# S5 recurrence of layer 0: two tokens per step, with half the phase table and a direct term

## The chip, the cores and the metric

The kernel runs on one core of one Trainium2 chip. The metric is the device time of one execution in microseconds (us). Before the change it is 1573.44 us, the median of three runs (1571.39, 1573.44, 1573.77).

## The reference, cut to what matters

Two layers of a decoder trunk on 256 tokens of width 1024, all in float32. The change touches one part of layer 0, the S5 mixer: 32 groups of 16 channels, each with 64 complex states.

```
dt = exp(log_dt); mag = exp(a_re * dt); abar = mag * (cos(a_im*dt) + i sin(a_im*dt))   # per group and state
bbar = ((abar - 1) / a) * b                                                            # 64 states x 16 channels
x[s] = abar * x[s-1] + bbar @ u[s]                                                     # s = 0..255, complex
y[s] = Re(c @ x[s]) + d_skip * u[s]
y    = gelu(y);  out = y * sigmoid(y @ w_glu + b_glu)
```

`u` is the last quarter of one combined input projection; its other three quarters are q, k and v of eight attention heads. The outputs of attention and S5 are concatenated and go into one output projection; a dense SwiGLU follows, then layer 1 (sparse attention and a mixture of eight experts).

## The kernel before, in words

Every engine has a queue of its own, written out by hand in program order, with semaphores between the queues. The 32 x 64 states lie as 16 channel tiles (`NCH`) of 128 partitions: two groups of 64 states each. PE is TensorE, DVE VectorE, ACT ScalarE, POOL GpSimd.

**Phase table.** The rotation of the state is taken out of the recurrence. `phase` holds cos and sin of s times the angle for each tile and token, 16 x 256 each. DVE builds it in eight doublings, `level(0)` to `level(7)` (L2185 to L2194, six operations each); a doubling needs the next power of the rotation, which POOL squares in `power(n)`. In the middle of the last doubling DVE computes the modulation (`columns`) and half of the first normalised input `uT` (`norm_first_out`); ACT does the other half.

**Weights.** POOL forms `b_bar`, ACT spreads it and c block-diagonally into `b_pad` and `c_pad`, PE transposes these (`s5_transposes`, 16 transposes of 128 x 128, before the projection), and ACT copies the results to `s5_bT` and `s5_cT` (`s5_weights`).

**The stage of the recurrence.** PE's order: `s_proj(0..3)` projects the S5 inputs (16 channels x 8 groups = 128 rows each, 256 tokens); then eight blocks, each with six matmuls of the q, k, v projection (`qkv`, 128x512), `drive` of two tiles, and `read_out` of the two tiles before. For each tile j:

- `drive(j)` on PE: 2 matmuls (real and imaginary) of a 32-row slice of the input, 256 tokens, to one PSUM bank (three banks in turn);
- `turn(j)` on DVE: two multiplies of 128x512 by the phase, an add and a subtract (the rotation back), and two scans over 256 tokens with factor `mag`;
- on POOL: two multiplies of 128x512 by the phase (L818), the rotation forward;
- `read_out(j)` on PE: 4 matmuls of 128 rows to 32 output rows, 256 tokens; those of two tiles alternate and lie in different column strips of the array.

`y_before_gelu(t)` on DVE adds `d_skip * u` for four tiles at once. DVE also does the rotary part of q and k (`rope0`) between turns. After the last block PE transposes q and k (`qk_transposes`), computes the first scores (L958), then `read_out(14)`, more scores, and `glu()` (L1127), which waits for the gelu of all four y tiles on ACT.

In the profile each float32 matmul of this stage stands as two records; a transpose stands as one. x8 at the drive is thus four matmuls.

## Time and profile before

| | |
|---|---|
| median of three runs | 1573.44 us |
| span of the profiled execution | 1566.3 us |
| what lies around the span, against that median | 7.1 us |
| PE busy in the span | 1489.2 us (95%) |
| DVE busy | 1288.4 us (82%) |
| ACT busy | 1027.9 us (66%) |
| POOL busy | 113.8 us (7%) |
| mean granted clock of PE | 0.986 of full |

The span is the time from the first to the last instruction that the hardware profiler recorded; the shares are of it. The table says nothing of single stages. The stage that the change touches runs from about 43 us to 137 us of the span.

### The profile page before, as it was taken

Reading aid. Unit: us, or ns where it says so; the run is one execution under the profiler, and the core shown is the slowest. Engines: PE = TensorE matmul, PEld = TensorE weight load, DVE = VectorE, ACT = ScalarE, POOL = GpSimd, SP = SyncE. Lnnn points to the kernel's source line nnn. Section 1 sums busy time; section 2 is a strip of 40 time slices with the busy share of each in tenths; the row PEclk is TensorE's granted clock in tenths of the full one; section 3 lists DMA queues with packets and bytes.
Section 4 is the critical chain, followed back from the end, with each engine's and each line's share of the span. In section 5 each row is a group of like instructions: output and inputs, shape, how many; then the busy total and the mean of one; then the engine's idle time right before and its main releaser. Section 6 shows DMA issues by size and latency. Waiting matters only on the chain.

```text
span 1566.3 us, 21687 instructions
## 1 busy us (share of the span) xinstructions
PE 1489.2 (95%) x7201; PEld 1160.6 (74%) x7202; DVE 1288.4 (82%) x1776; ACT 1027.9 (66%) x1325; POOL 113.8 (7%) x112
## 2 busy tenths in 40 slices
PE   3999999999899899999999999999999999999987
PEld 1645468888795478878888888888888888888865
DVE  6896458785586369899999999989989989989987
ACT  3104444443456457887787788787888888888765
POOL 5251000000000000000001001001001001001030
PEclk9899999999899999999999999999999999999998
DMA  9733968874564289999999999999999999999960
GB/s 309 274 108 138 386 253 294 310 257 161 190 215 164 106 315 392 389 339 386 386 348 384 390 346 379 389 356 373 384 358 373 385 365 368 387 365 367 383 232 28
DMA packets 209930, 482.81 MB, mean 308 GB/s; under 512 B 8084, under 2 KB 14534, under 8 KB 209750
## 3 DMA queue, kind: packets, MB, share of 16 engines
q1 hardware_dynamic: 205872, 468.91, 81.3%
q0 software_dynamic: 3360, 12.10, 2.1%
q10 hardware_dynamic: 646, 1.16, 0.3%
q8 instruction: 27, 0.44, 0.1%
q14 instruction: 25, 0.20, 0.0%
HBM read 474.27 MB, written 7.86 MB: 308 GB/s over the span
## 4 chain that ended last, share of the span: by engine, by line
PE 80%; DVE 5%; ACT 4%; issue 2%; DVEq 0%; ACTq 0%
PE ps L864 23%; PE ps L866 23%; PE ps L865 23%; PE ps L870 3%; DVE w_lo L2056 3%; PE ps L1399 2%; PE ps L1156 2%; ACT work L1947 1%; PE ps L889 1%; ACT w_hi L1686 1%; PE ps L1127 0%; PE ps L958 0%; PE ps L1345 0%; ACT uT L1699 0%; PE ps L984 0%
## 5 line engine op out<-in xcount | busy, mean ns | idle before, releaser
L2056 DVE TENSOR_TENSOR w_lo<-ring,w_hi 128x1024 fp32r<-128x1024 f32 (+2 forms) x572 | 676.5, 1214 | 80.6 <-ACT w_hi L1686 61.7
L1686 ACT ACTIVATE w_hi<-ring 128x1024 fp32r<-128x1024 f32 (+2 forms) x572 | 596.0, 1052 | 222.6 <-PE ps L866 220.6
L864 PE MATMUL ps<-w_hi,e_hi 128*128 128x512 f32 x896 | 356.2, 398 | 5.5 <-DVE w_lo L2056 5.5
L866 PE MATMUL ps<-w_hi,e_lo 128*128 128x512 f32 x896 | 349.5, 390 | 0.0
L865 PE MATMUL ps<-w_lo,e_hi 128*128 128x512 f32 x896 | 348.8, 389 | 0.0
L2056 DVE TENSOR_TENSOR w_lo<-ring_more,w_hi 128x1024 fp32r<-128x1024 f32 x192 | 232.1, 1223 | 16.0 <-ACT w_hi L1686 7.0
L1686 ACT ACTIVATE w_hi<-ring_more 128x1024 fp32r<-128x1024 f32 x192 | 202.7, 1060 | 47.6 <-PE ps L866 47.6
L864 PEld LDWEIGHTS ps<-w_hi,e_hi 128*128 128x128 f32 x896 | 168.3, 188 | 42.1 <-DVE w_lo L2056 9.6
L866 PEld LDWEIGHTS ps<-w_hi,e_lo 128*128 128x128 f32 x896 | 168.1, 188 | 36.1
L865 PEld LDWEIGHTS ps<-w_lo,e_hi 128*128 128x128 f32 x896 | 168.5, 188 | 32.7
L864 PE MATMUL ps<-w_hi,eT_hi 128*128 128x512 f32 x448 | 176.7, 395 | 12.6 <-DVE w_lo L2056 12.6
L866 PE MATMUL ps<-w_hi,eT_lo 128*128 128x512 f32 x448 | 174.6, 390 | 0.0
L865 PE MATMUL ps<-w_lo,eT_hi 128*128 128x512 f32 x448 | 174.5, 390 | 0.0
L864 PEld LDWEIGHTS ps<-w_hi,eT_hi 128*128 128x128 f32 x448 | 84.0, 188 | 35.5 <-DVE w_lo L2056 18.7
L864 PE MATMUL ps<-w_hi,x_hi 128*128 128x512 f32 (+4 forms) x272 | 99.9, 367 | 4.6 <-DVE x_lo L2091 4.6
L866 PE MATMUL ps<-w_hi,x_lo 128*128 128x512 f32 (+4 forms) x272 | 98.7, 363 | 0.0
L865 PE MATMUL ps<-w_lo,x_hi 128*128 128x512 f32 (+4 forms) x272 | 98.5, 362 | 0.0
L866 PEld LDWEIGHTS ps<-w_hi,eT_lo 128*128 128x128 f32 x448 | 84.1, 188 | 17.9
L865 PEld LDWEIGHTS ps<-w_lo,eT_hi 128*128 128x128 f32 x448 | 84.2, 188 | 16.7
L864 PEld LDWEIGHTS ps<-w_hi,x_hi 128*128 128x128 f32 x272 | 51.6, 190 | 13.6 <-issue 6.7
L834 POOL DMA_INDIRECT y_rows<-work,y_index x7 | 27.9, 3988 | 430.7 <-DVE work L2634 430.7
L865 PEld LDWEIGHTS ps<-w_lo,x_hi 128*128 128x128 f32 x272 | 51.7, 190 | 7.0
(308 smaller groups left out, 1579.8 us busy)
## 6 DMA issues: line engine op xcount, KB each, us to landing
ring<-in_moe_w_gate SPq DMA_DIRECT2D x96, 1024.0 KB, 7.2
ring<-in_moe_w_up SPq DMA_DIRECT2D x80, 1024.0 KB, 7.2
ring<-in_moe_w_down SPq DMA_DIRECT2D x64, 1024.0 KB, 7.2
ring<-in_w_ada SPq DMA_DIRECT2D x24, 2048.0 KB, 12.6
ring_more<-in_moe_w_down SPq DMA_DIRECT2D x48, 1024.0 KB, 7.5
ring_more<-in_moe_w_up SPq DMA_DIRECT2D x32, 1024.0 KB, 7.6
ring_more<-in_moe_w_gate SPq DMA_DIRECT2D x16, 1024.0 KB, 7.6
ring<-in_ff_w_gate SPq DMA_DIRECT2D x5, 2048.0 KB, 8.2
```

The lines of the kernel that those rows point to most:

```text
L834: pool.indirect_dma_start(y_rows[:, :], bass.IndirectOffsetOnAxis(ap=y_index[:, 0:1], axis=0), y_sb, None).then_inc(y_stored, 16)
L864: mm(o, xh, wh, start=start, stop=False)
L865: mm(o, xh, wl, start=False, stop=False)
L866: return mm(o, xl, wh, start=False, stop=stop)
L870: return nc.tensor.transpose(o, i, ident[0:n, 0:n])
L889: w = mm(ps[bank][j:j + 32, :], c_col[:, k:k + 1].broadcast_to([P, 32]), ap[:, k, :], start=k < 4, stop=False, tile_position=(0, j))
L1156: w = mm(ps[2 * n + t][:, :], catT[:, k, t * P:(t + 1) * P], ap[:, k, :], start=k == 4, stop=k == 3)
L1399: w = mm(ps[4 + 2 * n + t][:, :], ctxT[:, k, t * P:(t + 1) * P], ap[:, k, :], start=k == 0, stop=k == KD - 1)
L1686: fn(w, src, ACT.Copy).then_inc(hi_ready, 1)
L1947: w = fn(x_e[:, k, :], ps[6 + i][:, (k % 4) * P:(k % 4 + 1) * P], ACT.Identity, scale=mod_a[:, 1, k:k + 1], bias=mod_b[:, 1, k:k + 1])
L2056: V.tensor_tensor(w_lo[0:n, c, 0:f], src, w_hi[0:n, c, 0:f].bitcast(F32), ALU.subtract).then_inc(lo_ready, 1)
```

## The change

The recurrence is written for two tokens at a time: x[2k+1] = A^2 x[2k-1] + (A B) u[2k] + B u[2k+1]. Only odd states are kept. Odd outputs are C x[2k+1] as before; even outputs are y[2k] = (C A) x[2k-1] + (C B) u[2k], whose second part is the "direct term".

- The phase table has 128 steps instead of 256, so seven doublings; `level(n)` takes the next power, `n + 1`. The modulation and `norm_first_out` stand behind the last doubling.
- Two channel tiles (j and j+4) go together: eight turns `jp` instead of 16. A turn on DVE has the same four operations of 128x512 elements in all, and four scans of 128 steps instead of two of 256. POOL's two multiplies per turn keep their size, and there are eight pairs instead of 16.
- `drive(jp)`: eight matmuls of 128 tokens, all in the same 32-row strip of the array (`s5_abT` on even inputs, `s5_bT` on odd ones). Blocks 0 to 5 issue one each.
- `read_out(jp0)` serves four channel tiles: 36 matmuls of 127 or 128 tokens, two column strips in turn. It is issued four times instead of eight.
- New: `s5_direct` on PE (eight matmuls of 128x128), copied out by four small operations of ACT; `ab_bar` on POOL and its copy `ab_pads` on ACT; eight more transposes; three C A weight tiles made on POOL (seven operations of 128x512).
- `s5_transposes` moves from ahead of `s_proj(0)` to behind `s_proj(1)`, with 24 transposes.

```diff
-        phase = phase_buf[:, :, :].rearrange("p a (b c) -> p a b c", b=NCH)
+        phase = phase_buf[:, 0, :].rearrange("p (a b c) -> p a b c", a=2, b=NCH)
...
             for n in range(5, NLEV - 1):
                 power(n)
...
+            for i, (x, y, op) in enumerate(((0, 1, ALU.subtract), (1, 0, ALU.add))):
+                mul(s5_t, f(AI), b_bar[:, y, :, :])
+                mul(ab_bar[:, i, :, :], f(AR), b_bar[:, x, :, :])
...
+            pool.wait_ge(s5_wT_ready, 5)
...
+            mul(ca_t, fw(AI), mci)
+            mul(ca[0], fw(AR), cr)
+            add(ca[0], ca[0], ca_t)
+            affine(ca[1], ca[0], -1.0, 0.0)
+            mul(ca_t, fw(AI), cr)
+            mul(ca[2], fw(AR), mci)
...
-                for i, bank in enumerate((5, 6, 7, 4)):
+                for i, bank in enumerate((5, 6, 7, 4, 5, 6)):
                     if i == 3:
                         pe.wait_ge(mod_ready, 1)
+                    if i == 4:
+                        pe.wait_ge(s5_pads, 12)
+                        pe.wait_ge(s5_wT_ready, 2)
...
             pe.wait_ge(part_ready, 4)
-            s5_transposes()
             pe.wait_ge(uT_ready, 8)
...
+            def s5_direct():
+
+                pe.wait_ge(s5_wT_ready, 5)
+                for t in range(4):
+                    o = ps[7][:, t * P:(t + 1) * P]
+                    mm(o, b_pad[:, 0, t, :], s5_cT[:, 0, t, :], start=True, stop=False)
+                    w = mm(o, b_pad[:, 1, t, :], s5_cT[:, 2, t, :], start=False, stop=True)
+                w.then_inc(k_done, 1)
...
+            def drive(jp):
...
+                for n, j in enumerate(j_pair(jp)):
+                    t, r = j // 4, slice(32 * (j % 4), 32 * (j % 4) + 32)
+                    u = halves_of(t, r)
+                    for i in range(2):
+                        o = bank[:, (2 * n + i) * HS:(2 * n + i + 1) * HS]
+                        mm(o, s5_abT[r, i, t, :], u[:, 0, :], start=True, stop=False, tile_position=(r.start, 0))
+                        w = mm(o, s5_bT[r, i, t, :], u[:, 1, :], start=False, stop=True, tile_position=(r.start, 0))
                 w.then_inc(bu_done, 1)
...
+            def read_out(jp0):
...
+                for n in range(2):
...
+                    for jp in pairs:
+                        r, o = at_(jp, 0)
+                        mm(o, s5_kT[:, t, r], halves_of(t, slice(0, P))[:, 0, :], start=True, stop=False, tile_position=(0, r.start))
+                    for i, (c, a, b) in enumerate(((0, 0, 0), (1, 1, 1), (2, 1, 0), (2, 0, 1))):
+                        for jp in pairs:
...
+                            mm(o, s5_caT[:, c, t, r], x[:, 0:HS - 1], start=False, stop=i == 3, tile_position=(0, r.start))
+                    for i, (c, a, b) in enumerate(((0, 0, 0), (1, 1, 1), (2, 1, 0), (2, 0, 1))):
+                        for jp in pairs:
...
+                            w = mm(o, s5_cT[:, c, t, r], x, start=i == 0, stop=i == 3, tile_position=(0, r.start))
...
             s_proj(0)
             s_proj(1)
+            s5_transposes()
             s_proj(2)
+            s5_direct()
             drive(0)
-            drive(1)
             s_proj(3)
             pending[0] = True
-            drive(2)
-            for jp in range(8):
-                for s in range(6 * jp, 6 * jp + 6):
+            drive(1)
+            for i in range(8):
+                for s in range(6 * i, 6 * i + 6):
                     qkv(s)
-                for j in (2 * jp + 3, 2 * jp + 4):
-                    if j < NCH:
-                        drive(j)
-                if jp:
-                    read_out(2 * jp - 2)
+                if i + 2 < NJP:
+                    drive(i + 2)
+                if i in (2, 4, 6):
+                    read_out(i - 2)
...
             scores_pair(0, qT, kT, 0, True)
-            read_out(NCH - 2)
+            read_out(NJP - 2)
...
-            for n in range(5, NLEV):
+            for n in range(5, NLEV - 1):
                 level(n)
+            columns(0, 0, 1, 4)
+            dve.wait_ge(mod_ready, 1)
+            norm_first_out()
...
+                for n, j in enumerate(j_pair(jp)):
+                    for i in range(2):
+                        w = V.tensor_tensor_scan(z[:, n, i, :], s5_p[:, MAG2, j:j + 1].broadcast_to([P, HS]), s5_v2[:, n, i, :],
+                                                 0.0, ALU.mult, ALU.add)
...
-            for j in range(NCH):
-                turn(j)
-                if j % 4 == 2 and j >= 6:
-                    y_before_gelu(j // 4 - 1)
-                if j in (7, 8, 12, 13):
-                    rope0({7: 0, 8: 1, 12: 2, 13: 3}[j])
+            for jp in range(NJP):
+                turn(jp)
+                if jp in (3, 4):
+                    rope0(jp - 3)
+                if jp == 6:
+                    y_before_gelu(0)
+                    y_before_gelu(1)
+                if jp in (6, 7):
+                    rope0(jp - 4)
             dve.wait_ge(tables_in, 16)
             mask_max(0, neg0)
             mask_max(1, neg0)
+            y_before_gelu(2)
             y_before_gelu(3)
```

PE's order at the start of the stage, before. The rows are the last modulation columns (x1), the transposes of the S5 weights, the S5 projection (`uT,ring`, 256 tokens), the drives (`ada,work`) and the first six `qkv` matmuls (`ring,uT`); here x4 counts matmuls.

```order
L903 MATMUL ps<-cst,ada 128x1 x8
L870 MATMUL ps<-cst,work 128x128 x16
L1018 MATMUL ps<-uT,ring 128x256 x24
L1054 MATMUL ps<-ada,work 128x256 x4
L1018 MATMUL ps<-uT,ring 128x256 x8
L1054 MATMUL ps<-ada,work 128x256 x2
L1036 MATMUL ps<-ring,uT 128x512 x6
```

The same place after the change; L1092 and L1093 are the first of the four pairs of `s5_direct`, and the last two rows the first of the four pairs of `drive(0)`.

```order
L948 MATMUL ps<-cst,ada 128x1 x8
L1062 MATMUL ps<-uT,ring 128x256 x16
L912 MATMUL ps<-cst,work 128x128 x16
L912 MATMUL ps<-cst,phase_buf 128x128 x8
L1062 MATMUL ps<-uT,ring 128x256 x8
L1092 MATMUL ps<-work 128x128
L1093 MATMUL ps<-work 128x128
...
L1115 MATMUL ps<-ada,phase_buf 128x128
L1116 MATMUL ps<-ada,work 128x128
```

The 16 transposes moved behind two thirds of the first projection, eight more and `s5_direct` came in, and only one drive stands ahead of the last projection.

PE's order in two consecutive blocks of the middle, before (L1067 is the read-out, to 32 rows).

```order
L1036 MATMUL ps<-ring,uT 128x512 x6
L1054 MATMUL ps<-ada,work 128x256 x4
L1067 MATMUL ps<-gate_row,work 32x256 x8
L1036 MATMUL ps<-ring,uT 128x512 x6
L1054 MATMUL ps<-ada,work 128x256 x4
L1067 MATMUL ps<-ada,work 32x256 x8
```

After, the block with the first read-out, from the last pair of its drive to the next block.

```order
L1115 MATMUL ps<-ada,phase_buf 128x128
L1116 MATMUL ps<-ada,work 128x128
L1137 MATMUL ps<-ada,work 32x128 x2
L1142 MATMUL ps<-ada,phase_buf 32x127 x8
L1147 MATMUL ps<-ada,work 32x128 x8
L1137 MATMUL ps<-ada,work 32x128 x2
L1142 MATMUL ps<-ada,phase_buf 32x127 x8
L1147 MATMUL ps<-ada,work 32x128 x8
L1080 MATMUL ps<-ring,uT 128x512 x6
```

The read-out of eight matmuls in every block became one of 36, half as long each, in every second block.

## Rows read from the trace of the kernel before

**Rows 1.** Windows of the span: busy time by engine, PE's granted clock, DMA.

```profile
64.00:128.00 64.00, 62.53 (x245) 28.13 (x244) 59.78 (x110) 3.15 (x6) 34.37 (x29) 1.00 0.29 99
```

**Rows 2.** PE's timeline: start, duration, line, operation, count, idle before and releaser.

```profile
62.93 1.12 PE L1054 MATMUL ps<-ada,work 32*128 32x256 f32 x4
63.99 5.42 PE L1036 MATMUL ps<-ring,uT 128*128 128x512 f32 x12
...
75.75 1.14 PE L1054 MATMUL ps<-ada,work 32*128 32x256 f32 x8
76.82 1.92 PE L1067 MATMUL ps<-ada,work 128*32 128x256 f32 x16
78.67 5.42 PE L1036 MATMUL ps<-ring,uT 128*128 128x512 f32 x12
84.02 1.14 PE L1054 MATMUL ps<-ada,work 32*128 32x256 f32 x8
...
102.35 1.12 PE L1054 MATMUL ps<-ada,work 32*128 32x256 f32 x4 [0.67 <-DVE work L2242]
...
128.28 1.92 PE L1067 MATMUL ps<-ada,work 128*32 128x256 f32 x16 [1.08 <-DVE work L2258]
```

**Rows 3.** PE's timeline ahead of the S5 projection.

```profile
39.95 3.58 PE L903 MATMUL ps<-cst,ada 128*128 128x1 f32 x16
43.39 3.65 PE L870 MATMUL ps<-cst,work 128*128 128x128 f32 x16
47.31 10.97 PE L1018 MATMUL ps<-uT,ring 128*128 128x256 f32 x48 [0.27 <-ACT uT L1661]
```

**Rows 4.** DVE's timeline: last doubling's second operation, and its half of uT.

```profile
42.73 2.28 DVE L2186 TENSOR_TENSOR phase_buf<-phase_buf,work 128x2048 f32<-128x2048 f32 x1
...
45.32 1.90 DVE L2075 TENSOR_SCALAR uT<-ps,mod_a,mod_b 128x256 f32<-128x256 f32 x4
```

**Rows 5.** Windows at the start of the stage, for PE's granted clock (third number from the end).

```profile
46.00:48.00 2.00, 1.73 (x7) 1.24 (x7) 2.00 (x4) 2.00 (x5) 0.00 (x0) 0.50 1.05 387
48.00:50.00 2.00, 2.00 (x11) 1.77 (x10) 1.97 (x2) 1.69 (x4) 0.00 (x0) 0.99 1.05 389
```

**Rows 6.** A later return to the full clock: PE's timeline row and a window.

```profile
564.41 0.60 PE L1434 MATMUL ps<-bias_rows,cst 128*128 128x8 f32 x2 [1.09 <-DVE bias_rows L2489]
```

```profile
570.00:571.00 1.00, 1.00 (x10) 1.00 (x10) 1.00 (x1) 0.38 (x2) 0.00 (x0) 0.86 1.05 399
```

**Rows 7.** PE's short matmuls elsewhere; the last row gives duration ns as min/median/max.

```profile
130.13 1.09 PE L870 MATMUL ps<-cst,work 128*128 128x128 f32 x8
...
151.19 0.88 PE L984 MATMUL ps<-uT,ada 128*64 128x128 f32 x12
152.00 1.05 PE L903 MATMUL ps<-cst,work 128*128 128x1 f32 x8
...
555.75 2.25 PE L1404 MATMUL ps<-cst 128*128 128x128 f32 x18
```

```profile
L1404 PE MATMUL ps<-cst x50: 275/275/561, 555.7 to 574.3; 128*128 128x128 f32 x50
```

**Rows 8.** Timelines of DVE (first turn) and POOL (one tile).

```profile
59.38 0.69 DVE L2239 TENSOR_TENSOR work<-ps,phase_buf 128x512 f32<-128x512 f32 x1 [3.10 <-PE ps L1054]
...
61.70 1.27 DVE L2249 TENSOR_TENSOR_SCAN work<-work 128x256 f32<-128x256 f32 x2
```

```profile
66.81 2.50 POOL L818 TENSOR_TENSOR ada<-work,phase_buf 128x512 f32<-128x512 f32 x2 [1.21 <-DVE work L2249]
```

**Rows 9.** Timelines of PE and DVE from the last read-out to the GLU.

```profile
134.32 1.92 PE L1067 MATMUL ps<-gate_row,work 128*32 128x256 f32 x16
136.19 0.93 PE L958 MATMUL ps<-ada 64*128 64x128 f32 x8
137.30 7.17 PE L1127 MATMUL ps<-work,ring 128*128 128x256 f32 x32 [0.18 <-ACT work L1749]
```

```profile
136.31 0.48 DVE L2258 SCALAR_TENSOR_TENSOR work<-ada,s_d,ps 128x256 f32<-128x256 f32 x1 [0.18 <-PE ps L1067]
```

More of the change, by code:

```diff
@@ L239, in trunk @@
         s5_v = W0.take(2, S)
-        s5_small = W0.take(10)
         powers = W0.take(NLEV, 2, NCH)
+        s5_kT = W0.take(4, P)
         WA = Region(ada, 6 * D)
@@ L257, in trunk @@
         pT = WU.take(2, KW)
-        phase = phase_buf[:, :, :].rearrange("p a (b c) -> p a b c", b=NCH)
+        phase = phase_buf[:, 0, :].rearrange("p (a b c) -> p a b c", a=2, b=NCH)
+        WS = Region(phase_buf[:, 1, :], SLOT)
+        s5_abT = WS.take(2, 4, P)
+        s5_caT = WS.take(3, 4, P)
+        ab_pad = WS.take(2, 4, P)
+        ab_bar = WS.take(2, NCH, C_S5)
         WI = Region(ada[:, 2 * 4 * S:2 * 4 * S + 2048], 2048)
@@ L296, in trunk @@
         late_in = sem("late_in")
-        fill = [sem(f"slot{i}_filled") for i in range(NS1)]
+        fill = [sem(f"slot{i}_filled") for i in range(NS0)]
         half_fill = [[sem(f"slot{i}_half{j}_filled") for j in range(2)] for i in range(NS1)]
@@ L775, in _ @@
             step(pool.memset(b_pad, 0.0))
+            step(pool.memset(ab_pad, 0.0))
+            step(pool.memset(s5_kT, 0.0))
             step(pool.memset(phase[:, 0, :, 0:1], 1.0))
@@ L1047, in drive, with halves_of @@
+            def halves_of(t, r):
+                return s_inT[r, t, :].rearrange("p (k l) -> p l k", l=2)
+            def drive(jp):
+                if jp == 0:
+                    pe.wait_ge(s5_wT_ready, 7)
                     pe.wait_ge(vs_ready, 1)
-                if j == 8:
+                if jp == 4:
                     pe.wait_ge(vs_ready, 2)
-                if j >= 3:
-                    pe.wait_ge(bu_used, j - 2)
-                r = slice(32 * (j % 4), 32 * (j % 4) + 32)
-                for i in range(2):
-                    w = mm(ps[(6, 4, 5)[j % 3]][:, i * S:(i + 1) * S], s5_bT[r, i, j // 4, :], s_inT[r, j // 4, :], start=True,
-                           stop=True, tile_position=(32 * (j % 4), 0))
@@ L1056, in drive @@
[L1056 to L1070 removed]
+                if jp >= 3:
+                    pe.wait_ge(bu_used, jp - 2)
@@ L1729, in _, with s_in_out @@
             norm_first_out()
-            s5_weights()
-            act.wait_ge(s5_pads, 8)
-            for i in range(2):
+            ab_pads()
+            act.wait_ge(s5_pads, 12)
+            def s_in_out(i):
                 act.wait_ge(proj_done, 1 + i)
                 fn(s_inT[:, 2 * i:2 * i + 2, :], ps[2 + i][:, :].rearrange("p (c s) -> p c s", c=2), ACT.Copy).then_inc(vs_ready, 1)
+            s_in_out(0)
+            s5_weights(range(7))
+            s5_direct_out()
+            s_in_out(1)
             for i in range(4):
@@ L2238, in turn @@
                 step.wait()
[L2239 to L2242 removed]
+                chained(V.tensor_tensor(rotB, bu, phase_of(1, jp), ALU.mult))
+                chained(V.tensor_tensor(bu, bu, phase_of(0, jp), ALU.mult))
@@ L2243, in turn @@
+                step(V.tensor_tensor(s5_v2[:, :, 0, :], bu[:, :, 0, :], rotB[:, :, 1, :], ALU.add))
+                V.tensor_tensor(s5_v2[:, :, 1, :], bu[:, :, 1, :], rotB[:, :, 0, :], ALU.subtract).then_inc(bu_used, 1)
                 step.wait()
-                dve.wait_ge(bu_used, j + 1)
-                if j >= 2:
-                    dve.wait_ge(post_ready, j - 1)
-                z = zbuf[:, j % 2]
-                for i in range(2):
-                    w = V.tensor_tensor_scan(z[:, i, :], s5_p[:, MAG, j:j + 1].broadcast_to([P, S]), s5_v[:, i, :],
-                                             0.0, ALU.mult, ALU.add)
-                    if i == 0:
-                        step(w)
+                dve.wait_ge(bu_used, jp + 1)
@@ L2253, in turn @@
+                if jp >= 2:
+                    dve.wait_ge(post_ready, jp - 1)
+                z = zbuf[:, jp % 2]
+                for n, j in enumerate(j_pair(jp)):
+                    for i in range(2):
+                        w = V.tensor_tensor_scan(z[:, n, i, :], s5_p[:, MAG2, j:j + 1].broadcast_to([P, HS]), s5_v2[:, n, i, :],
+                                                 0.0, ALU.mult, ALU.add)
+                        if (n, i) != (1, 1):
+                            step(w)
                 w.then_inc(z_ready, 1)
-                dve.wait_ge(z_ready, j + 1)
+                dve.wait_ge(z_ready, jp + 1)
```

145 lines of the change are left out of this document (86 added, 59 removed).

## The prediction

> **What bounds the kernel now.** I read the windows by stage first, then PE's timeline in the stage of the recurrence, then DVE's and ACT's beside it. In the 64 us of [rows 1] PE is busy 62.53 us and DVE 59.78 us. Both look full, and the page alone would let one believe that DVE's scans set the pace. PE's timeline decides it: each group of six `qkv` matmuls is followed at once by a drive, that by a read-out, that by the next six [rows 2]. From 63.99 us, where the blocks begin, to 130.13 us [rows 7], where the q transposes follow the last read-out of the blocks, PE waited twice: 0.67 us for a PSUM bank and 1.08 us for y [rows 2]. That is all that DVE costs there: 1.75 us. So PE's own work is the bound, and DVE is a little less than full beside it. What the change takes from DVE gives at most those 1.75 us; what it adds to PE counts in full.
>
> Ahead of the stage, the projection starts at 47.31 us and waits for `uT` [rows 3]. DVE's half of `uT` runs from 45.32 us, after an operation of the last doubling that ends at 42.73 + 2.28 = 45.01 us [rows 4]; but the modulation columns were summed at 39.95 + 3.58 = 43.53 us [rows 3]. So the last doubling holds the path for about 1.5 us. Its other operations lie behind `uT` and beside PE's projection.
>
> **Prices.** A drive of two tiles costs PE 76.82 - 75.75 = 1.07 us, that of a single tile 63.99 - 62.93 = 1.06 us [rows 2]. Two tiles cost no more than one: they lie in different 32-row strips and run side by side. A read-out costs 78.67 - 76.82 = 1.85 us for 16 records in two column strips, that is eight steps of 0.23 us [rows 2]. So four records of a single drive stream for 0.92 us, and about 0.14 us goes to the change of shape.
>
> No row shows a 128-token float32 matmul in a 32-row or 32-column strip. The nearest is the full-array one: 18 records in 2.25 us, the last of which alone lasts 0.275 us, so (2.25 - 0.275) / 17 = 0.116 us each [rows 7]. That is half of 0.23, so the weight load still hides at 128 tokens. In column strips of 64 the step is (152.00 - 151.19) / 6 = 0.135 us, change of shape included [rows 7]. The lower bound is half of 0.23 less its fixed part, about 0.107; the upper bound inside this mechanism is 0.135. I take 0.116. A transpose costs (1.09 - 0.27) / 7 = 0.117 us [rows 7].
>
> **The change on PE, term by term.**
>
> - Transposes. The 16 old ones ran from 43.39 to 47.04 us, while PE would have waited for `uT` anyway: they cost nothing there. Behind `s_proj(1)` they are on the path: 16 x 0.117 = +1.9 us. The eight new ones: +0.9 us. They need two weight copies of ACT first; these take about as long as the first 16, so I add no wait.
> - `s5_direct`: eight matmuls, 16 records x 0.116 = +1.9 us.
> - Drives. Before: six pairs at 1.07 and four single ones at 1.06, together 10.7 us without the wait. After: each of the eight has 16 records in one row strip, so nothing runs side by side: 16 x 0.116 + 0.14 = 2.0 us, together 16.0. Difference +5.3 us. Tokens streamed are the same; the strips that ran together are lost.
> - Read-outs. Before 8 x 1.85 = 14.8 us. After 36 matmuls in two column strips make 18 steps of two records: 36 x 0.116 + 0.1 = 4.3 us, four times 17.2. Difference +2.4 us; the direct term is what is added.
> - The two waits for DVE: -1.75 us. DVE then has eight turns of some 3.6 us (61.70 + 1.27 - 59.38, [rows 8]; four scans of 128 for two of 256, which even at twice the price of a step leave a turn under 5 us), against a block of PE of 7 to 12 us. Banks come free long before the drive that reuses them.
> - Start of the projection: -1.45 us, from 47.31 to about 45.9 us, as the modulation starts at 43.6 instead of 45.05.
> - Clock. PE's granted clock is 0.50, the 1.2 GHz level, when the projection starts, and back at the full level at 48.0 us [rows 5]: the 0.7 us at half cost 0.35. Before, PE had worked without a gap from about 40 us to then. Now it stands idle from 43.5 to 45.9 us. After such a gap at the half level it worked from 564.41 us to about 570.3 us until the clock came back, 5.9 us [rows 6]. I take 4.7 us, between 0.7 and 5.9 but nearer to the row with a gap: 2.35 us lost instead of 0.35, +2.0 us. With the earlier start together: +0.55 us (from -1.4 to +1.2).
> - End. Only the last read-out now completes y(2) and y(3), so two additions and two gelus stand behind it instead of one; the chain from its end at 136.19 to the GLU at 137.30 [rows 9] grows by one addition less its overlap, +0.4 us.
>
> Off the path: POOL's C A tiles are seven operations at 2.50 / 2 = 1.25 us [rows 8], about 9 us, ready long before the first read-out, some 36 us behind `s_proj(1)`. POOL's `ab_bar` and ACT's copies end before the projections do. DVE's first doublings start about 1 us later, as they need the next power; the slack behind the shorter table takes it. The two DMA queues carry nothing new, and PE waits for no load in the stage. If POOL's C A were not covered, the first read-out would stall PE by what is missing, up to 9 us.
>
> Sum: 1.9 + 0.9 + 1.9 + 5.3 + 2.4 - 1.75 + 0.55 + 0.4 = +11.6 us. Everything behind the GLU is shifted by that and not changed; PE is as full there. The profiled span of 1566.3 us becomes 1577.9, and with the 7.1 us that the median of the runs has over that span, **1585.0 us**, 0.7% slower.
>
> **A rule against the row.** The single drive speaks for hidden loads: four records with 128-column weights in one row strip in 1.06 us [rows 2], while 128-column loads with next to no stream are spaced up to 1.05 / 8 = 0.13 us [rows 7]; were load and stream in series, the four would take 4 x (0.12 + 0.23) = 1.4 us. The Trainium skill, "TensorE: Matmul & The Clock Gate", Part 3, says that a weight load overlaps matmuls in flight only when its row group differs, while its Part 2 also allows the background weight buffer. By Part 3 the new drives, all in one row group, would pay every load; that is the first rival.
>
> **Rivals.**
>
> 1. *Loads in series in one row strip.* With half the stream per load there is less to hide it behind. Each record of a drive then costs 0.116 + 0.12 = 0.24 us, a drive 3.9 us, eight of them 15 us more: about 1600 us. Against it: the 1.06 us row and the 0.116 us row. Chance 0.08.
> 2. *Faster: the small tiles run beside the `qkv` matmuls.* The drives and read-outs take a quarter of the array. If PE's queue overlapped them with the full-array matmuls, their columns would cost little and DVE's 59.78 busy us in [rows 1] would have been the pace; halving its turns would let the blocks close up to their `qkv` part, by up to 15 us, about 1560 us. It decides from the point where more than 12 us of the 33 us of drives and read-outs is hidden. Against it: each drive and read-out pushes the next `qkv` group by its full length [rows 2]. Chance 0.04.
> 3. *No change.* Part of the same overlap, or 7 us and more of added work in PE's idle moments around the start. PE has only some 2 us idle there. Chance 0.04.
> 4. *Clock at half through all the transposes.* If it came back only behind them, the projections and the 24 transposes would lose about 3 us more than I took: 1588 us. Inside the range.
>
> **How the numbers follow.** The forecast has a chance of 0.84, including the fourth rival. Its own range: with 0.107 us a record 2 us less, with 0.135 us 5 us more, the start from -2 to +3 us, and 1 us for the median of a few runs: 1580 to 1592. I put the range at 1579 to 1593. A measurement of this kernel can tell about 0.2%, 3 us. Faster: 0.04 and a remainder, 0.05. Same: 0.04. Slower: 0.91.
>
> **What the profile of the changed kernel would show.** Each drive 2.0 us from its start to the next group (3.9 if the first rival holds); each read-out 4.3 us; the `qkv` groups still 5.35 us; PE without waits between the blocks, while DVE waits for PE before most turns; the projection starting at about 45.9 us with the clock at 0.50 for some us; the GLU starting near 149 us instead of 137.30. The prediction is wrong if `qkv` groups start before the drive ahead of them has had its time, if a drive costs near 1.1 us, or if DVE's turns still stand ahead of waiting PE work.

## The result and the profile after

The changed kernel took 1582.17 us (median of five runs, 1576.90 to 1585.69), the kernel before 1573.44 us (1571.39 to 1573.77). The ratio is 1.0056, with a 95% interval of 1.0038 to 1.0074: slower by 0.6%. The forecast was 1585.0 us with a range of 1579 to 1593.

| | before | after |
|---|---|---|
| median | 1573.44 us | 1582.17 us |
| profiled execution: time / span | not listed / 1566.3 us | 1584.64 / 1582.8 us |
| PE busy | 1489.2 us | 1505.6 us |
| DVE busy | 1288.4 us | 1247.0 us |
| mean granted clock of PE | 0.986 | 0.980 |
| start of the GLU of layer 0 | 137.30 us [rows 9] | 147.79 us |

DVE lost 41 us of work in the whole span and the kernel became slower. The windows of the changed kernel say why at once; the columns are those of [rows 1]:

```profile
46.00:48.00 2.00, 2.00 (x5) 1.64 (x6) 0.00 (x0) 1.37 (x4) 0.00 (x0) 0.50 1.04 385
48.00:50.00 2.00, 2.00 (x6) 1.55 (x6) 0.00 (x0) 0.00 (x0) 0.00 (x0) 0.50 1.05 389
50.00:52.00 2.00, 2.00 (x9) 1.73 (x8) 0.00 (x0) 0.00 (x0) 0.00 (x0) 0.84 1.04 385
...
64.00:128.00 64.00, 64.00 (x369) 40.57 (x368) 35.54 (x87) 3.83 (x9) 20.64 (x18) 1.00 0.29 99
```

In the last row DVE's work fell from 59.78 to 35.54 us, and PE went from 62.53 us to all of the 64. The first three answer to [rows 5]: the clock is at 0.50, the 1.2 GHz level, from the start of the projection until 50 + 2 x (1 - 0.84) / 0.5 = 50.64 us.

PE's timeline of the changed kernel, from the modulation columns to the GLU (L948 columns, L912 transposes, L1062 projection, L1092 and L1093 direct term, L1115 and L1116 drive, L1080 `qkv`, L1137 to L1147 read-out, L1206 GLU):

```profile
39.76 2.25 PE L948 MATMUL ps<-cst,ada 128*128 128x1 f32 x16
45.94 9.47 PE L1062 MATMUL ps<-uT,ring 128*128 128x256 f32 x32 [3.94 <-issue]
55.24 1.91 PE L912 MATMUL ps<-cst,work 128*128 128x128 f32 x16
57.23 1.07 PE L912 MATMUL ps<-cst,phase_buf 128*128 128x128 f32 x8
58.13 3.62 PE L1062 MATMUL ps<-uT,ring 128*128 128x256 f32 x16
61.59 0.38 PE L1092 MATMUL ps<-work 128*128 128x128 f32 x2
...
63.46 0.49 PE L1115 MATMUL ps<-ada,phase_buf 32*128 32x128 f32 x2
...
65.47 3.72 PE L1062 MATMUL ps<-uT,ring 128*128 128x256 f32 x16
...
71.13 5.42 PE L1080 MATMUL ps<-ring,uT 128*128 128x512 f32 x12
76.48 0.49 PE L1115 MATMUL ps<-ada,phase_buf 32*128 32x128 f32 x2
...
78.48 5.42 PE L1080 MATMUL ps<-ring,uT 128*128 128x512 f32 x12
...
93.19 0.42 PE L1137 MATMUL ps<-ada,work 128*32 128x128 f32 x4
93.45 1.03 PE L1142 MATMUL ps<-ada,phase_buf 128*32 128x127 f32 x16
94.31 1.04 PE L1147 MATMUL ps<-ada,work 128*32 128x128 f32 x16
...
97.25 1.12 PE L1080 MATMUL ps<-ring,uT 128*128 128x512 f32 x2
...
146.28 0.93 PE L1003 MATMUL ps<-ada 64*128 64x128 f32 x8
147.79 2.42 PE L1206 MATMUL ps<-work,ring 128*128 128x256 f32 x10 [0.59 <-ACT work L1852]
```

A piece of work costs the time from its start to the start of the next piece. A drive is 65.47 - 63.46 = 2.01 us, and again 78.48 - 76.48 = 2.00; the `qkv` group is still 76.48 - 71.13 = 5.35 us; a read-out is 97.25 - 93.19 = 4.06 us for twice 4 + 16 + 16 = 72 records. No piece of the blocks has a wait ahead of it. It is DVE that waits now. The list of DVE's waits has this for the first operation of its turn (us in total, times, longest; the longest is the first, ahead of the blocks):

```profile
DVE work L2339 <- PE ps L1116: 44.5, 8, 19.8
```

Ahead of the projection, DVE's timeline of the changed kernel:

```profile
38.44 1.63 DVE L2289 TENSOR_TENSOR phase_buf<-phase_buf,ada 128x1024 f32<-128x1024 f32 x1
40.10 1.23 DVE L2290 TENSOR_TENSOR ada<-phase_buf,work 128x1024 f32<-128x1024 f32 x1
...
42.50 1.23 DVE L2292 TENSOR_TENSOR phase_buf<-phase_buf,ada 128x1024 f32<-128x1024 f32 x1
43.64 0.15 DVE L2149 COPY mod_b<-ps 128x8 f32<-128x8 f32 x1
...
43.91 1.90 DVE L2178 TENSOR_SCALAR uT<-ps,mod_a,mod_b 128x256 f32<-128x256 f32 x4
```

The columns were summed on PE at 39.76 + 2.25 = 42.01 us, but DVE came to them only at 43.64, when its last doubling was done. So DVE, not the columns, still held the path. Beside its doublings POOL did the new work for `ab_bar` (L769, L833), which lasted until 37.40 + 1.58 = 38.98 us:

```profile
35.84 1.49 POOL L769 TENSOR_TENSOR phase_buf<-work,ada 128x256 f32<-128x256 f32 x1
37.40 1.58 POOL L833 TENSOR_TENSOR phase_buf<-phase_buf,ada 128x256 f32<-128x256 f32 x1
```

DVE's operations of 128x1024 beside these took 1.53, 1.64 and 1.63 us, the two behind them 1.23 and 1.22. The kernel before has no such work on POOL, and 1.22 us for this size.

**The numbers behind the GLU.** The GLU starts 10.49 us later. The profiled span is 16.5 us longer and the medians differ by 8.7 us. What lies behind the GLU took 1566.3 - 137.30 = 1429.0 us before and 1582.8 - 147.79 = 1435.0 after, at a lower mean clock. The same kernel repeats that spread: the five runs of the changed kernel have spans of 1575.1 to 1583.9 us at clocks of 0.988 to 0.980. The start of the GLU is the sharper measure of each edit, and each experiment gives both.

It has a spread of its own, for it is read from one execution of each kernel. The changed kernel and three of its edited versions below (drives by twos, read-out of four strips, DVE padded) have the same code up to the end of the first 32 projection records; that end comes at 55.24, 55.64, 54.72 and 55.31 us, as the clock comes back sooner or later. Three traces (the kernel before and its two edited versions) have the same code up to the first block. In them the 48 projection records start within 0.05 us of each other and take 10.97, 12.24 and 13.20 us, and the first block starts at 63.99 us (the trace of [rows 2]), 65.20 and 66.19 us. So the GLU of the changed kernel is known to about 1 us and that of the kernel before to about 2, and the trace of the kernel before that was read for the prediction was the luckiest of the three. That fits a median that moved by 8.7 us where the GLU moved by 10.49.

### The profile page after: what moved, and what is told of

Read it like the earlier page. It is cut to its first block, busy times and chain, and to the rows that moved or that the text cites. A ratio compares the mean times of both kernels' runs of the same rounds, so it can differ in the third digit from the quotient of the medians.

```text
span 1582.8 us, 22130 instructions
## 1 busy us (share of the span) xinstructions
PE 1505.6 (95%) x7449; PEld 1183.5 (75%) x7450; DVE 1247.0 (79%) x1738; ACT 1031.8 (65%) x1335; POOL 108.7 (7%) x112
## 4 chain that ended last, share of the span: by engine, by line
PE 86%; DVE 5%; ACT 4%; issue 2%; DMA 1%; SPq 1%; DVEq 0%; ACTq 0%
PE ps L906 23%; PE ps L908 22%; PE ps L907 22%; PE ps L912 3%; PE ps L1080 3%; DVE w_lo L2159 3%; PE ps L1478 2%; PE ps L1235 2%; PE ps L934 1%; ACT work L2050 1%; DMA ring<-in_w_ada 1%; PE ps L1062 1%; SPq L658 1%; ACT w_hi L1782 1%; PE ps L1115 1%
## 5 line engine op out<-in xcount | busy, mean ns | idle before, releaser
L906 PE MATMUL ps<-w_hi,eT_hi 128*128 128x512 f32 x448 | 177.7, 397 | 10.8 <-DVE w_lo L2159 10.8
L908 PEld LDWEIGHTS ps<-w_hi,x_lo 128*128 128x128 f32 x272 | 52.3, 192 | 7.3
```

Source lines behind the costliest of these rows:

```text
L906: mm(o, xh, wh, start=start, stop=False)
L908: return mm(o, xl, wh, start=False, stop=stop)
```

## The experiments

My theory: PE's own work sets the pace of the stage, DVE has slack after the change, and the time lost lies in small matmuls that use one row strip (drives) or two column strips (read-outs) where more could run side by side. The rivals: DVE's turns, or a wait hidden in PE's row, set the pace; and, for the start of the stage, that the clock after PE's gap, not DVE's doublings, is what costs.

All but two experiments (the kernel before with DVE padded, and with a read-out of four strips) edit the changed kernel. Each stands beside fresh runs of the kernel before, whose medians were 1573.04, 1572.85 and 1574.09 us in the three sets.

| | median | ratio to before, 95% | GLU starts |
|---|---|---|---|
| drives by twos | 1570.70 us | 0.9998, 0.9979 to 1.0016 | 139.39 us |
| transposes ahead | 1579.38 us | 1.0042, 1.0022 to 1.0062 | 145.25 us |
| read-out of four strips | 1572.88 us | 1.0004, 0.9986 to 1.0022 | 139.06 us |
| all three | 1558.83 us | 0.9922, 0.9898 to 0.9947 | 128.23 us |
| changed kernel, DVE padded | 1581.25 us | 1.0050, 1.0031 to 1.0069 | 147.85 us |
| before, DVE padded | 1581.06 us | 1.0051, 1.0029 to 1.0072 | 147.44 us |
| fill in the gap | 1580.89 us | 1.0051, 1.0033 to 1.0070 | 147.69 us |
| all three, `uT` first | 1556.38 us | 0.9884, 0.9864 to 0.9905 | 124.95 us |
| before, read-out of four strips | 1579.96 us | 1.0047, 1.0030 to 1.0065 | 148.42 us |

### Drives by twos

Two turns' drives are issued together, their matmuls in turn, so that neighbours lie in different row strips and different banks.

```diff
-            def drive(jp):
+            def drive(*jps):
...
-                for n, j in enumerate(j_pair(jp)):
...
-                        mm(o, s5_abT[r, i, t, :], u[:, 0, :], start=True, stop=False, tile_position=(r.start, 0))
-                        w = mm(o, s5_bT[r, i, t, :], u[:, 1, :], start=False, stop=True, tile_position=(r.start, 0))
+                for n in range(2):
+                    for i in range(2):
+                        for k, (wT, first) in enumerate(((s5_abT, True), (s5_bT, False))):
+                            for jp in jps:
+                                j = j_pair(jp)[n]
...
+                                w = mm(o, wT[r, i, t, :], halves_of(t, r)[:, k, :], start=first, stop=not first,
+                                       tile_position=(r.start, 0))
...
-            drive(0)
+            drive(0, 1)
             s_proj(3)
-            drive(1)
...
-                if i + 2 < NJP:
-                    drive(i + 2)
+                if i in (0, 2, 4):
+                    drive(i + 2, i + 3)
```

> The changed kernel with its drives issued in twos, the matmuls of two turns in different 32-row strips alternating, nothing else. My theory (PE's own work is the bound, and the drives lost their side-by-side strips): two drives take the 2.0 us of one, so 8 us leave the stage; the GLU starts at about 139.8 us of the span instead of 147.79, and the time falls from 1582 to about 1574. Rival (weights or the order of the queue set the price, not the strips): two drives take 4 us and nothing changes. Rival (DVE paces the stage): nothing changes.

PE's timeline of this kernel, with the columns and the projection first, and four records in a row of the drives where the changed kernel has two:

```profile
38.36 1.95 PE L948 MATMUL ps<-cst,ada 128*128 128x1 f32 x16
...
46.05 9.75 PE L1062 MATMUL ps<-uT,ring 128*128 128x256 f32 x32 [5.74 <-ACT uT L1758]
...
63.85 0.50 PE L1116 MATMUL ps<-ada,phase_buf 32*128 32x128 f32 x4
...
65.86 3.72 PE L1062 MATMUL ps<-uT,ring 128*128 128x256 f32 x16
```

Two drives take 65.86 - 63.85 = 2.01 us, exactly what one took. Four calls instead of eight save 8.0 us; the GLU comes 147.79 - 139.39 = 8.40 us earlier, although the first 32 projection records had ended 0.4 us later than in the changed kernel. So the drives' excess was the lost side-by-side work, as the prediction had it. The Trainium skill, "TensorE: Matmul & The Clock Gate", Part 3, also has it that tiles in different strips run at once, and this run agrees with that.

The first two rows bear on the start of the stage: here the columns were summed at 40.31 us, 1.7 us earlier than in the changed kernel, and the projection started at 46.05 all the same. The columns are not what it waits for.

### Transposes ahead

```diff
+            s5_transposes(range(4))
             pe.wait_ge(uT_ready, 8)
...
             s_proj(1)
-            s5_transposes()
+            s5_transposes((4, 5))
```

ACT's first five weight copies move ahead of its pads with them.

> The changed kernel with the 16 old transposes back ahead of the wait for uT. My theory: 1.9 us leave the path, and as PE works on through the gap, its clock comes back earlier than at 50.6 us, worth up to 2 us more: the GLU at 144 to 146 us. If the gap does not matter for the clock, only the 1.9 us: 145.9 us. Rival (the transposes were hidden where they are now): GLU stays at 147.8.

The projection now runs from 46.01 to 54.70 us and the eight remaining transposes follow; the GLU comes 2.54 us earlier than in the changed kernel. The 16 moved transposes had cost 1.99 us in the timeline above (57.23 - 55.24), the rest is the clock: the windows from 46, 48 and 50 us read 0.63, 0.52 and 1.00 where the changed kernel has 0.50, 0.50 and 0.84, which is 2 x (0.13 + 0.02 + 0.16) = 0.6 us. That those 0.6 us are the work of the edit is not shown: the next kernel has nothing changed ahead of the projection, and its first 32 records take 54.72 - 46.07 = 8.65 us, against 8.69 here and 9.30 in the changed kernel.

### Read-out of four strips

```diff
-                pairs = (jp0, jp0 + 1)
+                pairs = range(jp0, jp0 + 4)
...
-                if i in (2, 4, 6):
-                    read_out(i - 2)
+                if i == 2:
+                    read_out(0)
...
-            read_out(NJP - 2)
+            read_out(NJP - 4)
```

The wait for `post` grows from `jp0 + 2` to `jp0 + 4` turns. One call now covers four channel tiles, in all four column strips.

> The changed kernel with its four read-outs of two column strips made two read-outs of all four strips, same matmuls. My theory: a read-out's 18 steps take as long with four tiles as with two, 4.1 us, so two read-outs less, 8.1 us: GLU at about 139.7 us and about 1574 us. If the issue of 288 instructions is slower than the steps, a read-out takes up to 6 us and the gain is 4 us. Rival (PE waits for four turns of DVE and POOL before the read-out): a wait of several us ahead of the read-outs, and no gain.

The GLU comes 8.73 us earlier. Two calls of 4.06 us are 8.1 of them; 0.52 us stood already at the end of the first 32 projection records, ahead of anything edited. A row that shows such a read-out stands with the next experiment.

### All three

The three edits above together.

> The changed kernel with drives in twos, read-outs of four strips and the 16 transposes ahead of the wait for uT. If the terms add as PE's own work: 8 + 8.1 + 1.9 and up to 2 us less than the changed kernel, the GLU at 128 to 130 us of the span against 137.3 in the kernel before, and a time of 1564 to 1566 us, 0.5% under the kernel before. If DVE, POOL or the issue of PE become the bound once PE's work shrinks, the stage stops near the kernel before, GLU at 134 us or later.

PE's timeline of this kernel, the first row of a read-out of four strips and the `qkv` behind it; then its window for the stage:

```profile
86.25 0.43 PE L1141 MATMUL ps<-ada,work 128*32 128x128 f32 x8
...
90.31 1.99 PE L1082 MATMUL ps<-ring,uT 128*128 128x512 f32 x4
```

```profile
64.00:128.00 64.00, 62.34 (x525) 36.27 (x523) 39.05 (x101) 8.45 (x16) 20.03 (x16) 1.00 0.36 125
```

The read-out of twice the matmuls takes 90.31 - 86.25 = 4.06 us, the same as that of two strips. The three edits alone moved the GLU by 8.40 + 2.54 + 8.73 = 19.67 us, together by 147.79 - 128.23 = 19.56: they add up, as parts of a queue do when it alone is the bound. (To 0.1 us is luck, at a spread of about 1 us.) With them the halved recurrence is 0.8% faster than the kernel before. The time came out lower than expected: the median is 14.2 us under that of the kernel before, while the GLU starts only 137.30 - 128.23 = 9.07 us earlier. Where the other 5 us lie is open. PE executes exactly the same matmuls as in the changed kernel; only their order and neighbours differ.

### The changed kernel, DVE padded

The first multiplication of each turn is done three times: 8 x 2 more operations of 0.72 us, 11.5 us in all.

```diff
+                chained(V.tensor_tensor(rotB, bu, phase_of(1, jp), ALU.mult))
+                chained(V.tensor_tensor(rotB, bu, phase_of(1, jp), ALU.mult))
                 chained(V.tensor_tensor(rotB, bu, phase_of(1, jp), ALU.mult))
```

> The changed kernel with the first multiply of each turn on DVE issued three times instead of once: 16 more operations of 0.7 us, 11.6 us more on DVE in the stage, same results. My theory (PE is the bound and what DVE saves is slack): the GLU stays at 147.8 us and the time at 1582, within noise. Rival (DVE's turns pace the stage): 11 us later, 1593 us.

Its window for the stage:

```profile
64.00:128.00 64.00, 64.00 (x370) 40.60 (x369) 46.04 (x98) 3.89 (x9) 19.98 (x17) 1.00 0.28 99
```

DVE works 46.04 us instead of 35.54 in this window, and the GLU moves by 0.06 us. DVE does not bound the changed kernel; it has at least these 11.5 us of slack.

### The kernel before, DVE padded

The same 11.5 us (16 turns, one more operation each) in the kernel before.

```diff
+                chained(V.tensor_tensor(rotB, bu, c(1), ALU.mult))
                 chained(V.tensor_tensor(rotB, bu, c(1), ALU.mult))
```

> The kernel before with the first multiply of each of its 16 turns issued twice: 11.5 us more on DVE. This prices the slack that DVE had before. DVE was busy 59.8 of 64 us and PE waited 1.75 us for it in the stage, so I expect DVE to become the bound here: 6 to 9 us more, about 1580 us. If DVE had been the pace already, 11.5 us more, 1585 us; if its slack was larger than I read it, no change.

Two rows of PE's timeline and the window of the stage:

```profile
47.26 12.24 PE L1018 MATMUL ps<-uT,ring 128*128 128x256 f32 x48 [1.31 <-ACT uT L1661]
...
108.33 2.07 PE L1054 MATMUL ps<-ada,work 32*128 32x256 f32 x4 [4.59 <-DVE work L2243]
```

```profile
64.00:128.00 64.00, 59.41 (x218) 27.16 (x216) 60.63 (x109) 3.16 (x6) 32.50 (x26) 0.92 0.29 99
```

The GLU moves by 147.44 - 137.30 = 10.14 us. Of these, 65.20 - 63.99 = 1.21 us stood already at the first block, ahead of anything edited: the 48 projection records took 12.24 us instead of 10.97 [rows 3], as the clock came back later. The 11.5 us of work thus cost about 8.9 us, and the median moved by 8.2, at the upper end of what was expected. PE waits, and its clock falls: the drive behind the 4.59 us wait takes 2.07 us instead of 1.1. So before the change DVE had some 2.6 us of slack behind PE, known to about 2 us. The two directions are not alike: 11.5 us more on DVE cost about 9 us, and 24 us less gave back only the 1.75 us for which PE had waited [rows 2] and 1.06 us more, as the account of the prediction shows.

### Fill in the gap

Five dummy matmuls between the columns and the wait for `uT`, to hold the clock.

```diff
+            for _ in range(5):
+                mm(ps[5][:, 0:P], ident, ident, start=True, stop=True)
             pe.wait_ge(uT_ready, 8)
```

> The changed kernel with five dummy matmuls of 128x128 on PE between the modulation columns and the wait for uT, to an unused bank; they fill some 2 us of the gap. It asks what the gap alone costs through the clock. My theory: the granted clock is back to full earlier than at 50.6 us, and the first projection (45.94 to 55.24 us) ends up to 1.5 us earlier. Rival (the gap does not matter, or the dummies run past uT): no change or up to 0.5 us later.

PE's timeline and a window of this kernel:

```profile
40.03 1.36 PE L1055 MATMUL ps<-cst 128*128 128x128 f32 x10
46.61 8.70 PE L1064 MATMUL ps<-uT,ring 128*128 128x256 f32 x32 [5.22 <-ACT uT L1759]
```

```profile
46.00:48.00 2.00, 1.39 (x3) 1.17 (x4) 0.52 (x2) 1.93 (x6) 0.00 (x0) 0.50 1.03 383
```

The dummies end at 41.4 us, 5.22 us ahead of the projection, and the clock is at half all the same when it starts. The GLU moves by 0.10 us. DVE's doublings ran about 0.7 us later in this execution, already before the dummies, so that the projection started at 46.61 us instead of 45.94; in return the clock was back 3.25 us after that start, where it took 4.7 us in the changed kernel. Without dummies it took from 3.4 us (read-out of four strips) to 5.3 us (drives by twos). So no gain of the burst is shown, and one of under about 1 us is not ruled out. The gain of up to 1.5 us at the projection's end that was expected did not come: it ended at 55.14 us instead of 55.24.

### All three, uT first

The kernel with all three edits, and DVE's last doubling placed behind the columns and the first norm's output.

```diff
-            for n in range(5, NLEV - 1):
-                level(n)
+            level(5)
             columns(0, 0, 1, 4)
             dve.wait_ge(mod_ready, 1)
             norm_first_out()
+            level(6)
```

> The version with drives in twos, read-outs of four strips and the transposes ahead of uT, and in addition the modulation columns and uT ahead of the last doubling of the table instead of behind it. My theory: in the changed kernel it was DVE's doublings (up to 43.6 us) and no longer PE's columns (done near 40.2 us when the clock is full) that held uT; moved, the projection starts at 42.5 to 43 us instead of 46.1, or when its weights land, and the GLU at about 125 us instead of 128.23; time 1555 to 1556 us. Rival (the weights of the projection land only near 46 us): no gain. Rival (the last doubling, now later, delays the first turn): a wait of DVE's table ahead of the first turn.

PE's timeline of this kernel, then DVE's, then POOL's (L769 and L833 of 128x256 are the last of `ab_bar`):

```profile
41.91 1.95 PE L912 MATMUL ps<-cst,work 128*128 128x128 f32 x16
44.41 7.17 PE L1064 MATMUL ps<-uT,ring 128*128 128x256 f32 x32 [0.56 <-ACT uT L1760]
51.42 1.04 PE L912 MATMUL ps<-cst,phase_buf 128*128 128x128 f32 x8
```

```profile
42.15 0.17 DVE L2153 COPY mod_b<-ps 128x8 f32<-128x8 f32 x1 [6.64 <-PE ps L949]
...
46.63 1.23 DVE L2293 TENSOR_TENSOR phase_buf<-phase_buf,ada 128x1024 f32<-128x1024 f32 x1
47.89 1.95 DVE L2294 TENSOR_TENSOR ada<-phase_buf,work 128x1024 f32<-128x1024 f32 x1
49.77 2.06 DVE L2295 TENSOR_TENSOR phase_buf<-phase_buf,work 128x1024 f32<-128x1024 f32 x1
```

```profile
36.07 0.62 POOL L769 TENSOR_TENSOR phase_buf<-work,ada 128x256 f32<-128x256 f32 x1
36.77 0.72 POOL L833 TENSOR_TENSOR phase_buf<-phase_buf,ada 128x256 f32<-128x256 f32 x1
46.92 1.84 POOL L769 TENSOR_TENSOR work<-work 128x512 f32<-128x512 f32 x1 [9.43 <-issue]
48.84 1.91 POOL L769 TENSOR_TENSOR phase_buf<-work 128x512 f32<-128x512 f32 x1
...
54.60 1.05 POOL L769 TENSOR_TENSOR work<-work 128x512 f32<-128x512 f32 x1
```

The projection starts 1.5 us earlier than in the changed kernel, and takes 51.42 - 44.41 = 7.01 us where that took 55.24 - 45.94 = 9.30, at the full clock from its first matmul: PE's gap had shrunk to 0.56 us. The GLU comes 3.28 us before that of the kernel with three edits: 1.70 us by the start of the projection and 1.58 by its clock. This is the best version: 1556.38 us, 1.2% faster than before. DVE's doublings had thus held the projection in the changed kernel, and the clock behind the gap came with them. The start was expected at 42.5 to 43 us and came at 44.41: now the columns hold it, and DVE waited 6.64 us for them.

The rows of POOL show what had made the doublings slow. With DVE idle, the last two operations of `ab_bar` take 0.62 and 0.72 us; in the changed kernel, beside the doublings, they take 1.49 and 1.58. DVE's 128x1024 takes 1.22 us where POOL is idle and up to 1.64 beside them.

### The kernel before, read-out of four strips

Is it the four strips alone that gain, without the halved recurrence?

```diff
-                pe.wait_ge(post_ready, j0 + 2)
+                pe.wait_ge(post_ready, j0 + 4)
...
-                    for j in (j0, j0 + 1):
+                    for j in range(j0, j0 + 4):
...
-                if jp:
-                    read_out(2 * jp - 2)
+                if jp in (2, 4, 6):
+                    read_out(2 * jp - 4)
...
-            read_out(NCH - 2)
+            read_out(NCH - 4)
```

> The kernel before with its eight read-outs of two column strips made four read-outs of all four, in every second block. PE's work falls by 4 x 1.85 = 7.4 us, as it does in the changed kernel with the same edit. My theory: here DVE has almost no slack (59.8 us busy of 64), and POOL holds only four results, so PE waits for turns instead: little or no gain, 1570 to 1578 us. Rival (PE's work alone decides in this kernel too): 7 us less, 1566 us.

PE's timeline of this kernel, two drives and the last read-out (L1067):

```profile
96.07 1.29 PE L1054 MATMUL ps<-ada,work 32*128 32x256 f32 x4 [2.29 <-DVE work L2242]
...
107.23 2.07 PE L1054 MATMUL ps<-ada,work 32*128 32x256 f32 x4 [1.98 <-DVE work L2242]
...
144.07 0.41 PE L1067 MATMUL ps<-ada,work 128*32 128x256 f32 x2 [3.69 <-POOL gate_row L818]
```

Four calls of read-out are gone, some 7.4 us of PE, and the GLU comes 148.42 - 137.30 = 11.12 us later, 2.20 us of it from the projection ahead of the blocks (13.20 us for its 48 records instead of 10.97), which the edit does not touch. The median is 5.9 us higher, so the loss is real, and larger than expected (1570 to 1578 us). PE reached DVE's banks too early: it waited 2.29, 1.98 and 1.72 us for them. Each such wait also splits a pair of drives that had run side by side, 1.06 us each time, and the clock fell to a mean of 0.92 from 64 to 128 us (the drive at 107.23 takes 2.07 us), some 5 us. The last read-out needs four tiles from POOL instead of two and waits 3.69 us. In these kernels the strips paid only together with the shorter turns of DVE. The shorter turns with one of the two reorderings (drives by twos, or four strips) came out level with the kernel before, and ahead of it only with more.

## Why the prediction came out as it did

The verdict, the mechanism and the range held. Step by step, the predicted term and what the traces show:

- PE is the bound: right. No wait is left in the blocks, and 11.5 us more on DVE move nothing. "That is all that DVE costs there: 1.75 us" was read too low. The wait of 0.67 us split a pair of drives, whose halves lie at 100.56 and 102.35 us; side by side they would have cost 1.07 us together and cost 1.06 each. DVE thus held PE up by 2.8 us. The sum is unharmed, since it counts these two among the four single drives.
- Transposes, +2.8 us: 58.13 - 55.24 = 2.89 us. Direct term, +1.9: 63.46 - 61.59 = 1.87 us.
- Drives, 2.0 us each, +5.3: 2.01 us, +5.4.
- Read-outs, 4.3 us each, +2.4: 4.06 us, so 4 x 4.06 - 14.8 = +1.4. This is the term that was mis-sized most. I took 0.116 us for each of 36 steps, from matmuls in the full array [rows 7]. The measured step is 4.06 / 36 = 0.113 us with the changes of shape inside, and between two rows above eight steps take 94.31 - 93.45 = 0.86 us, 0.107 us each: the lower bound was the right price.
- Start and clock, +0.55: the projection starts at 45.94 us (45.9 predicted) and has half the clock for 50.64 - 45.94 = 4.7 us (4.7 taken). The sum is right and two steps behind it are not. I wrote that the modulation columns, summed at 43.53 us, would be what comes last, with DVE free for them. In fact the columns were summed at 42.01 us and DVE was busy until 43.64. Two things moved: PE's clock came back while the columns ran, and DVE's doublings took up to 1.64 us an operation where 1.22 us stands in the kernel before. The second is the cost of POOL's `ab_bar`, which I had put off the path because it ends before the projections do: it slowed the six operations of DVE that ran beside it by 2.2 us together, by their durations against the same operations in the kernel before (no run moved `ab_bar` itself). That two errors met at the same microsecond is luck. Two runs show that the doublings held the path: with the drives by twos the columns came 1.7 us earlier and the projection did not; with `uT` ahead of the last doubling it started 1.5 us earlier. The other step is the clock before the change. I took the 0.7 us at half of [rows 5] for a property of that kernel; in the two other traces with its code up to there, the half level lasted 3.3 and 5.2 us of the projection. In them the columns took 1.95 us instead of 3.58, and PE then waited 2.5 and 3.7 us in all ahead of the projection, so the gap that I gave to the change alone stood there too. Against those the change would have lost 0.7 us by the clock, or gained 0.3, instead of losing 2.0. That 2.0 came out in the pair of traces is luck too.
- End, +0.4: from the last read-out's end to the GLU it is 147.79 - 146.28 = 1.51 us, before 1.11 us [rows 9]; +0.40.

With the measured terms the sum is -1.37 + 1.98 + 2.89 + 1.87 + 5.4 + 1.4 - 1.75 + 0.40 = +10.8 us (the first two are the start and the clock), against 10.49 us measured and 11.6 predicted. The medians moved by 8.7 us, and the lucky clock of the trace before, 1.2 to 2.2 us, is the likely difference. The step from there to a time was weak: the 7.1 us added for what lies around the span was mostly not that. In the changed kernel 1584.64 - 1582.8 = 1.8 us lies around it, so the profiled execution of the kernel before must have been some 5 us quicker than its median. It cancelled only because that median was used on both sides. From the median plus 10.5 us one gets 1583.9 us; the remaining 1.8 us are inside the spread of the granted clock. The parts of the stated range add up to 1580 and 1594, not 1592; nothing hangs on it.

The rivals: *loads in series in one row strip* would have made a drive 3.9 us; it is 2.01. The Trainium skill, "TensorE: Matmul & The Clock Gate", Part 3, has a load overlap matmuls in flight only when the row group differs; 16 records in one row group at 2.01 us speak against that for this shape. *Small tiles beside `qkv`* is out too: each `qkv` group starts when the drive ahead has had its time. *No change* is out as well: the GLU moved by 10.49 us, well beyond the spread of 1 to 2. *Clock at half through all the transposes*: it was back at 50.64 us, before them.

What the prediction did not see is where the gain would lie. It said of the drives that the strips that ran together are lost, and stopped there. The loss was not part of the mathematics of the change, only of the order in which its matmuls were written.

The 6.0 us behind the GLU in the profiled execution need no cause in the change. The kernel with the filled gap has the same code behind the GLU and took 1574.1 - 147.69 = 1426.4 us there, less than the 1429.0 of the kernel before, at a mean clock of 0.990.

Open: why the medians of the two fastest versions lie 14.2 and 17.7 us under the kernel before, where their GLUs start 9.07 and 12.35 us earlier. The mean clocks of their runs are 0.982 to 0.990, those of the kernel before beside them 0.981 to 0.990, mostly 0.982 to 0.985.

## What to carry to other kernels

What the relief of an engine is worth stands in the waits of the engine that it holds up and in what these waits break up, here 1.75 and 1.06 us. Its busy share does not tell it, nor does padding it, which measures slack in the other direction alone (11.5 us more on DVE cost about 9 us, 24 us less gave 2.8). For small matmuls count the strips that run side by side: the order of issue sets it, and the same matmuls in another order (drives by twos, read-outs of four strips) moved the GLU by 8.4 + 8.7 = 17 us. Here two engines were both nearly full and had to be relieved together: each of the two reliefs alone (the halved turns, the four strips) made the kernel slower, by 0.6% and 0.5%. Both, with the drives by twos and the transposes ahead, made it 0.8% faster, and with `uT` first 1.2%. Work that is added to an engine with time to spare can still slow another one that lies on the path, as POOL's `ab_bar` did to DVE. And a stretch at the half clock that one trace shows should be looked for in a second execution before it goes into a sum: here it lasted 0.7, 3.3 and 5.2 us for the same code.

## What the runs showed of the hardware

- A read-out of 144 records in four column strips takes 4.06 us, one of 72 records in two strips also 4.06 us. Two drives in two row strips take 2.01 us, one takes 2.01.
- DVE and POOL slow each other. DVE's 128x1024 operation takes 1.22 us alone, and 1.95 and 2.06 us while POOL multiplies 128x512; POOL's takes 1.05 us alone, and 1.84 and 1.91 us in the same stretch. POOL's 128x256 takes 0.62 us with DVE idle and 1.49 us beside DVE's 128x1024, which then takes up to 1.64. The slowing in both directions is shown; how it comes about is not. The Trainium skill, "SBUF — State Buffer", section "SBUF: two separate sides", has these two engines share one pair of ports, held by one operation at a time when DVE has two inputs in SBUF and POOL reads SBUF too. The rows agree with it roughly. DVE's operation that began first, at 46.63 us, still took 1.23 us, and POOL's that began at 46.92 grew by 0.79 us, where DVE's lasted 0.94 us longer. DVE's next grew by 0.73 us, where POOL's lasted 0.87 us longer. No run tests it against another way of sharing.
- After PE's gaps of 3.9 us and of 5.2 us the projection began at the 1.2 GHz level; after one of 0.56 us it ran at 2.4 GHz throughout. Ten dummy records of 1.36 us at the head of the gap made no difference that the spread would show.
- The moment at which the clock comes back differs between executions of the same code: 0.7, 3.3 and 5.2 us after the start of the projection in the kernel before, 3.4 to 5.3 us in the changed one.
- Runs of one and the same kernel spread by up to 10.2 us (1575.94 to 1586.10 us in the kernel with the filled gap), and their mean granted clock goes with it: 0.990 for the shortest and 0.982 for the longest.
